# Group-norm rows, fox groups, state matmuls and merged rows put at other places of one unit order

## The chip, the cores and the metric

The kernel runs as one program on one core of a Trainium2 chip. The metric is device time of the execution in microseconds (us), lower is better. The engines of the core are called here as the profile calls them: PE (TensorE, matmul), PEld (its weight loads), DVE (VectorE), ACT (ScalarE), POOL (GpSimd) and SP (SyncE, which issues all DMAs of this kernel).

## The reference, cut to what matters

Two different blocks run one after the other on 256 tokens of width 1024, each two layers deep.

```python
def first_block(...):                      # per layer
    proj = h @ w_in[layer]                 # x_bc, z, dt, q, k, v, ... , gates
    y_a = mamba2_branch(...)               # state-space scan, then grouped_rms_norm
    y_b = sliding_window_branch(...)       # "swa"
    y_c = forgetting_attention_branch(...) # "fox": scores + cum[q] - cum[k], causal softmax
    merged = sum_i sigmoid(gate_i) * (y_i @ w_proj[layer, i])
    x = x + merged @ w_out[layer]
def merge_branches(...):                   # second block, per layer
    y = g_a * (o_attn @ w_br_attn) + g_p * (pool @ w_br_pool) + g_f * (fourier @ w_br_four)
    return y @ w_out
def conv_ffn(h, w_up, conv_w, w_down): ...
```

## The kernel before, in words

**Arithmetic.** Every large product is made of float32 rounded to its high part and the remainder: `W = hi + lo`, `x = xh + xl`, and three matmuls (`hi*xh`, `hi*xl`, `lo*xh`; L797 to L799 when the weights stand still, L810 to L812 when tokens do). Weights come as half chunks of 128x1024. SP loads a half chunk into one of seven `raw` buffers (L728), ACT copies it into `hi` (L1145), and DVE (L1454) or POOL (L1925) subtracts to get `lo`. There are five `hi`/`lo` pairs (`NS = 5`), so the `split` of half chunk i+5 stands in the order next to the matmuls that read half chunk i, and ACT's copy waits until PE has used half chunk i. A chunk for 256 tokens is 48 matmuls.

**Order.** One Python object writes a list of units by hand. All five engines walk this same list, each does its own part of each unit, in order, and waits by semaphore. `gemm` appends: the split of a later half chunk, the matmul unit, another split, and then one `tick()`. A tick advances every generator in `self.side` by one step; this is how the narrow work (attention groups, state-space groups, group norm) is laid between the weight chunks. So a unit that waits on one engine holds all that stands behind it in the list on that engine, the weight splits too.

**What the change touches.** The fox generator `attn("fox", l, g)` takes eight ticks: `fox_prep` at 0, `scores` 2, `exp` 3, `probs` 4, `turn` (transposes of the probabilities) 6, `pv` 7. Before, group g was appended after its v chunk, so groups 0 to 3 start at ticks 3, 6, 9 and 12 of the layer (tick 0 is the first q chunk; q, k and v chunks fill ticks 0 to 11, the eight conv chunks 12 to 19). In `fox_prep` SP first waits for the splits that stand before it in the list (it must issue their successors' loads in order), then issues a broadcast read `t_A<-cu_scratch` of 512 KB (L748); POOL waits for it and does two subtractions (L1932, L1933) and two selects (L1919). Groups use two buffers in turn.

State-space groups (`ssm`) start at ticks 0, 2, 6 and 8 of a later stretch. `ssm0` copies, `ssm1` has exponentials on ACT and waits for a broadcast read too, `ssm2` is three multiplications on DVE (L1636, then L1640 twice), `ssm3` is the state matmul and its copy on ACT (L1267), `ssm4` the output matmuls (L966 to L968), which need that copy.

Group norm: `gnorm` puts four `gn` units on DVE (L1681 and L1685). Then `ysplit` rounds the rows of each chunk: ACT copies (L1285), DVE subtracts (L1675). The projection `proj` of branch 0 reads them (k rows 0-1 are of chunk 0, and so on). In that stretch the last swa groups still run: `exp` of group 3, `turn` and `pv` of groups 2 and 3 (L1240 and L1608 copy out the transposes, L933 is `pv`).

In the second block, `msplit2` rounds the eight rows of the merged sum (ACT L1407, DVE L1851) into `H2`, which the gate matmuls read until the last gate chunk has passed, so all wait for that. `wout2` reads them.

Of the kernel before, what the change touches and what calls it, by code (L numbers as in the profile page):

```python
# [152 lines left out]
class Order:  # L153
# [145 lines left out]
    def ssm(self, l, g):  # L299
        self.add("ssm0", l=l, c=g, s=(self.sbank(), self.sbank()))  # L300
        yield
        self.add("ssm1", l=l, c=g)
        yield
        self.add("ssm2", l=l, c=g)
        yield
        yield
        self.add("ssm3", l=l, c=g, s=(self.sbank(),))
        yield
        self.add("ssm4", l=l, c=g, s=(self.sbank(),))

# [51 lines left out]
    def gated_proj(self, l, br, perm, split):  # L362

        def gate(c):
            self.gemm("gate", l, c, wcols("w_in", l, O_G + br * 1024 + np.arange(c * 256, c * 256 + 256)), 8, 256, 256,
                      x=(br,))

        def proj(c):
            self.gemm("proj", l, c, wcols("w_proj", (l, br), np.arange(c * 256, c * 256 + 256), perm), 8, 256, 256,
                      x=(br,))  # L370
        gate(0)
        gate(1)
        proj(0)
# [12 lines left out]
    def layer1(self, l):
        b = self.rstd(l, (2, 1, 1) if l else (0, 1, 1))
        self.add("norm1", l=l, g=b, n=(self.half(0), self.half(1)))
        self.late_splits()
        self.small(l)  # L390
        self.share = False
        for g in range(4):
            for off, kind in ((O_QC, "q"), (O_KC, "k")):
                self.gemm(kind, l, g, wcols("w_in", l, off + np.arange(g * 256, g * 256 + 256)), 8, 256, 256)
            self.vproj(l, "vc", O_VC, g)
            self.side.append(self.attn("fox", l, g))
            if l == 1 and g == 1:
                self.add("ctx")
        for n, c in enumerate((4, 6, 5, 7, 0, 1, 2, 3)):
            if l == 1 and n == 4:  # L400
                self.side.append(self.squares(8))
            self.gemm("conv", l, c, wcols("w_in", l, O_XBC + np.arange(c * 256, c * 256 + 256)), 8, 256, 256,
                      then=lambda m: self.later("conv2", l=l, c=c) or ())
        self.drain()
        self.share = True
        self.side.append(self.staggered([self.ssm(l, g) for g in range(4)], (0, 2, 6, 8)))
        self.zgate(l, 2, O_ZC, None)
        for c in range(4):
            self.gemm("rope", l, c, wcols("w_in", l, O_QB + SWA_PERM[c * 256:c * 256 + 256]), 8, 256, 256,
                      then=lambda m: self.rope_then(l, c))  # L410
        self.gemm("rope", l, 4, wcols("w_in", l, O_KB + np.arange(256)), 8, 256, 256,
                  then=lambda m: self.rope_then(l, 4))
        self.vproj(l, "vb", O_VB, 0)
        rest = self.gated_proj(l, 2, None, False)
        next(rest)
        self.drain()
        self.side.append(self.staggered([self.attn("swa", l, g) for g in range(4)], (0, 2, 5, 7)))
        self.zgate(l, 0, O_ZA, None)
        for _ in rest:
            pass  # L420
        for c in range(4):
            self.add("ysplit", l=l, c=c, x=(0,))
        for _ in self.gated_proj(l, 0, None, False):
            pass
        self.drain()
        self.zgate(l, 1, O_ZB, SWA_PERM)
        for _ in self.gated_proj(l, 1, SWA_PERM, True):
            pass
        self.add("msplit", l=l, c=3)
        self.tick()  # L430
        self.some_mods(1)
        every, self.every = self.every, 0
        self.side.append(self.squares(l + 1))
        for c in range(4):
# [50 lines left out]
    def block2(self, l):  # L485
# [34 lines left out]
        for bi, nkt, wn, perm in ((1, 2, "w_br_pool_2", None), (2, 2, "w_br_four_2", None), (0, 4, "w_br_attn_2", LAT_PERM)):  # L520
            for c in range(4):
                self.gemm("gate2", l, c, wcols("w_in_2", l, 1280 + bi * 1024 + np.arange(c * 256, c * 256 + 256)), 8, 256,
                          tw, x=(bi, tw))
                if bi == 0 and c == 0:
                    self.drain()
                if bi == 0 and c == 3:
                    for k in range(6):
                        self.add("msplit2", l=l, c=k)
                self.gemm("proj2", l, c, wcols(wn, l, np.arange(c * 256, c * 256 + 256), perm), nkt, 256, tw,
                          x=(bi, tw, nkt, len(units)))  # L530
# [72 lines left out]
class Tiles:  # L603
# [78 lines left out]

    def attn(self, kind, l, g):

        o = (5120 if kind == "fox" else 2048) + 1536 * (g % 2)
        f = self.a if kind == "fox" else self.b
        t0 = f(o, 512).rearrange("p (h c) -> p h c", h=4)
        t1 = f(o + 512, 1024).rearrange("p (h c) -> p h c", h=4)
        base = self.ST[:, (g % 2) * 64:(g % 2) * 64 + 64]
        return t0, t1, [base[:, 8 * i:8 * i + 8] for i in range(5)]  # L690

    def ssm(self, g):
# [72 lines left out]
def tensor(e, units, t, M):  # L765
# [318 lines left out]
    def proj2(u):  # L1084
        bi, tw, nkt, n = u.x[2:]
        k0 = (0, 4, 6)[bi]
        chan(u, nkt, 256, tw, lambda k: t.Y2[:, k0 + k, 0:tw], lambda k: t.YL2[:, k0 + k, 0:tw],
             lambda k: at("y2", u.l, k0 + k), ("proj2mm", u.l))

    def wout2(u):  # L1090
        tw = 256 if u.l else 512
        chan(u, 8, 256, tw, *h2(tw), lambda k: at("m2", u.l, k), ("wout2mm", u.l))

    def ffup(u):
        tw = 256 if u.l else 512
# [29 lines left out]
def scalar(e, units, t, M):  # L1125
# [21 lines left out]
    def sq(u):  # L1147
        s = u.l
        tw, c0 = (256, 256) if s == 8 else (256, 0) if s == 3 else (TW[s], 0)
        for k in (u.c, u.c + 1):  # L1150
# [252 lines left out]

    def msplit2(u):
        tw = 256 if u.l else 512
        q.wait_ge(at("mg2", u.l, 0, u.c), at("h2mm", u.l, 0))
        act(t.H2[:, u.c, 0:tw], t.M2[:, u.c, 0:tw], ACT.Copy).then_inc(*up("act", ("m2h", u.l, u.c), ("m2", u.l, u.c), ("m2", u.l)))  # L1407

    def ffup(u):
        l, pr, vg, tw = u.l, u.c, u.x[2], 256 if u.l else 512  # L1410
# [27 lines left out]
def vector(e, units, t, M):  # L1438
# [409 lines left out]
    def msplit2(u):  # L1848
        tw = 256 if u.l else 512
        q.wait_ge(at("m2h", u.l, u.c))  # L1850
        tt(t.HL2[:, u.c, 0:tw], t.M2[:, u.c, 0:tw], t.H2[:, u.c, 0:tw].bitcast(F), ALU.subtract).then_inc(  # L1851
            *up("dve", ("m2", u.l, u.c), ("m2", u.l)))

    def xadd(u, s, j, k, ps):
# [59 lines left out]
def gpsimd(e, units, t, M):  # L1914
# [249 lines left out]
```

## Time and profile before

| what | value |
|---|---|
| median of 3 runs | 2228.97 us (2228.39 to 2231.36) |
| the profiled execution, own time | 2235.63 us |
| its span, first to last instruction | 2233.9 us |
| PE busy | 2100.3 us (94%) |
| PEld, DVE, ACT, POOL busy | 1865.8, 1258.7, 1107.3, 958.7 us |
| mean granted PE clock | 0.972 |
| HBM read | 327.08 MB, 147 GB/s over the span |

A busy PE is near the bound of the kernel, so what matters is the 6% in which it is not busy, and the stretches in which its granted clock is below 1.

### The profile page before, as it was taken

What the parts mean: (1) busy time and instruction counts of PE and PEld (TensorE: products, weight loads), DVE (VectorE), ACT (ScalarE), POOL (GpSimd) and SP (SyncE); (2) the same over time, 40 slices, a digit from 0 to 9 for tenths busy, and PEclk for the clock granted to TensorE, in tenths of its full rate; (3) what the DMA queues carried; (4) which work ended last, traced back from release to release, by engine and by line L of the source; (5) the groups of instructions that cost most, each with busy time, mean ns of one, the idle gap of its engine ahead of it and who ended that gap; (6) DMA issues with size and microseconds to landing.
All of it is one profiled execution on the core that took longest, in us unless ns stands there. A gap on an engine that the chain in (4) does not pass through costs nothing.

```text
span 2233.9 us, 36649 instructions
## 1 busy us (share of the span) xinstructions
PE 2100.3 (94%) x14868; PEld 1865.8 (84%) x14868; DVE 1258.7 (56%) x1902; ACT 1107.3 (50%) x1873; POOL 958.7 (43%) x426
## 2 busy tenths in 40 slices
PE   5999998999999998998999999899999979999997
PEld 5898997998998998996766787678888868898997
DVE  5576847336477655454276435555445546856665
ACT  4475466545575475544266323433333345646553
POOL 3564644563546644652111333323333333365663
PEclk9999999999999999998999999999999989999998
DMA  6445443566554543565112343433333313354551
GB/s 234 179 157 178 160 150 125 188 208 220 204 191 154 185 146 125 192 204 188 67 66 86 127 142 121 169 125 109 129 113 132 106 64 104 116 180 140 196 180 60
DMA packets 93176, 330.64 MB, mean 148 GB/s; under 512 B 10064, under 2 KB 13264, under 8 KB 92752
## 3 DMA queue, kind: packets, MB, share of 16 engines
q1 hardware_dynamic: 93008, 328.30, 42.7%
q8 instruction: 118, 1.93, 0.3%
q14 instruction: 50, 0.41, 0.1%
HBM read 327.08 MB, written 1.18 MB: 147 GB/s over the span
## 4 chain that ended last, share of the span: by engine, by line
PE 79%; DVE 10%; ACT 7%; issue 2%; POOL 1%; DMA 1%; SPq 0%; DVEq 0%; ACTq 0%; POOLq 0%
PE ps L797 22%; PE ps L798 21%; PE ps L799 21%; ACT t_hi L1145 2%; PE ps L844 2%; PE ps L810 1%; PE ps L811 1%; PE ps L812 1%; DVE t_lo L1454 1%; PE ps L933 1%; PE ps L1059 1%; PE ps L917 1%; DVE t_RB L1829 1%; PE ps L1069 1%; ACT t_B L1231 1%
## 5 line engine op out<-in xcount | busy, mean ns | idle before, releaser
L1925 POOL TENSOR_TENSOR t_lo<-t_raw,t_hi 128x1024 fp32r<-128x1024 f32 (+1 forms) x358 | 878.6, 2463 | 1078.6 <-ACT t_hi L1145 1070.5
L797 PE MATMUL ps<-t_RB,t_hi 128*128 128x256 f32 (+1 forms) x3712 | 1173.8, 316 | 20.5 <-DVE t_RB L1741 5.3
L798 PE MATMUL ps<-t_RB,t_hi 128*128 128x256 f32 (+1 forms) x3712 | 1151.2, 310 | 0.0
L799 PE MATMUL ps<-t_RB,t_lo 128*128 128x256 f32 (+1 forms) x3712 | 1150.5, 310 | 0.0
L797 PEld LDWEIGHTS ps<-t_RB,t_hi 128*128 128x128 f32 x3712 | 714.8, 193 | 94.2 <-issue 31.2
L798 PEld LDWEIGHTS ps<-t_RB,t_hi 128*128 128x128 f32 x3712 | 715.4, 193 | 34.9 <-issue 2.0
L799 PEld LDWEIGHTS ps<-t_RB,t_lo 128*128 128x128 f32 x3712 | 714.6, 192 | 35.8
L1145 ACT ACTIVATE t_hi<-t_raw 128x1024 fp32r<-128x1024 f32 (+1 forms) x506 | 524.5, 1042 | 426.9 <-PE ps L799 389.8
L1454 DVE TENSOR_TENSOR t_lo<-t_raw,t_hi 128x1024 fp32r<-128x1024 f32 x148 | 207.3, 1402 | 288.7 <-ACT t_hi L1145 288.5
L1884 DVE SCALAR_TENSOR_TENSOR t_A<-ps,t_V,t_A 128x510 f32<-128x510 f32 (+1 forms) x176 | 102.3, 612 | 154.6 <-ACT t_A L1415 153.1
L1415 ACT ACTIVATE t_A<-ps,t_V 128x512 f32<-128x512 f32 (+1 forms) x88 | 48.5, 577 | 125.9 <-PE ps L799 125.9
L810 PE MATMUL ps<-t_hi,t_RB 128*128 128x256 f32 (+1 forms) x320 | 94.9, 296 | 11.1 <-DVE t_RB L1741 7.2
L1857 DVE SCALAR_TENSOR_TENSOR t_X<-ps,t_MOD,t_X 128x256 f32<-128x256 f32 x168 | 72.0, 478 | 58.9 <-PE ps L799 58.9
L811 PE MATMUL ps<-t_hi,t_RB 128*128 128x256 f32 (+1 forms) x320 | 91.9, 287 | 0.0
L812 PE MATMUL ps<-t_lo,t_RB 128*128 128x256 f32 (+1 forms) x320 | 91.7, 287 | 0.0
L810 PEld LDWEIGHTS ps<-t_hi,t_RB 128*128 128x128 f32 x320 | 63.0, 197 | 18.1 <-DVE t_RB L1741 8.1
L1464 DVE TENSOR_TENSOR t_SQA<-t_SQA,t_NT 128x256 f32<-128x256 f32 (+1 forms) x63 | 52.6, 834 | 29.6 <-ACT t_NT L1166 26.0
L811 PEld LDWEIGHTS ps<-t_hi,t_RB 128*128 128x128 f32 x320 | 63.4, 198 | 0.3 <-issue 0.2
L812 PEld LDWEIGHTS ps<-t_lo,t_RB 128*128 128x128 f32 x320 | 63.3, 198 | 0.0
L1401 ACT ACTIVATE t_A<-ps 128x512 f32<-128x512 f32 (+1 forms) x48 | 22.4, 490 | 81.6 <-PE ps L799 78.3
L844 PE MATMUL ps<-t_raw,t_C 128*32 128x256 f32 x768 | 55.2, 409 | 4.7 <-DVE t_X L1857 2.6
L1427 ACT ACTIVATE t_RB<-t_A 128x512 fp32r<-128x512 f32 (+1 forms) x44 | 23.2, 526 | 70.6 <-DVE t_A L1899 70.6
(302 smaller groups left out, 2180.5 us busy)
## 6 DMA issues: line engine op xcount, KB each, us to landing
t_raw<-in_W SPq DMA_DIRECT2D x586, 512.0 KB, 3.5
t_A<-cu_scratch SPq DMA_DIRECT2D x8, 512.0 KB, 6.1
t_B<-cu_scratch SPq DMA_DIRECT2D x8, 512.0 KB, 4.7
t_raw<-in_W SPq DMA_DIRECT2D x16, 256.0 KB, 2.9
t_A<-in_C SPq DMA_DIRECT2D x2, 1536.0 KB, 8.6
t_X<-in_X SPq DMA_DIRECT2D x2, 512.0 KB, 4.4
t_X<-in_X SPq DMA_DIRECT2D x1, 1024.0 KB, 9.9
out<-t_X SPq DMA_DIRECT2D x1, 1024.0 KB, 4.8
```

What stands on the lines that cost most here:

```text
L797: mm(o, hi[:, w], xh(k), start=k == 0 and j == 0, stop=False)
L798: mm(o, hi[:, w], xl(k), start=False, stop=False)
L799: i = mm(o, lo[:, w], xh(k), start=False, stop=k == nkt - 1 and m == u.x[1] - 1)
L810: mm(o, xh(k)[:, r], hi[:, w], start=k == 0 and j == 0, stop=False)
L811: mm(o, xl(k)[:, r], hi[:, w], start=False, stop=False)
L812: i = mm(o, xh(k)[:, r], lo[:, w], start=False, stop=k == nkt - 1 and tb == blocks[-1])
L844: i = mm(b[32 * j:32 * j + 32, 0:256], t.C32[:, k, :], t.raw[r % NR][:, j * 256:j * 256 + 256], start=k < 4, stop=k >= 4)
L1145: act(t.hi[s][:, 0:w], t.raw[r][:, 0:w], ACT.Copy).then_inc(*up("act", ("hi", u.i), ("split", u.i)))
L1454: tt(t.lo[s][:, 0:w], t.raw[r][:, 0:w], t.hi[s][:, 0:w].bitcast(F), ALU.subtract).then_inc(*up("dve", ("split", u.i)))
L1857: stt(out=x, in0=ps[:, z * 256:z * 256 + 256], scalar=t.modv(u.l, j, k, z), in1=x, op0=ALU.mult, op1=ALU.add).then_inc(*up("dve", ("x", s, ...
L1884: return stt(out=o[:, :, r], in0=ps[:, :, s], scalar=cw, in1=o[:, :, r], op0=ALU.mult, op1=ALU.add)
L1925: tt(t.lo[s][:, 0:w], t.raw[r][:, 0:w], t.hi[s][:, 0:w].bitcast(F), ALU.subtract).then_inc(*up("pool", ("split", u.i)))
```

## The change

Five edits of the order and of places in memory, no edit of the arithmetic:

1. The four `ysplit` units of branch 0 stood together ahead of gate chunk 0. Now rows 0 and 1 stand after gate chunk 0 and rows 2 and 3 after gate chunk 1, both ahead of projection chunk 0.
2. Fox groups start at ticks 4, 6, 9 and 11 (before 3, 6, 9 and 12). Group 2 gets a third buffer, in `RS` and `NT`, and the small sums move to fit; the buffer of group g is now waited for as that of group g-3.
3. `ssm3` stands one tick earlier; `ssm4` keeps its tick.
4. `msplit2` of rows 0 and 1 goes ahead of projection chunk 2 of the attention branch, 2 to 5 ahead of chunk 3. Rows 0 to 3 are written to `Y2`/`YL2` places 4 to 7 (pool and Fourier rows lay there), so they wait only for branch 2 to be done.
5. Squares of tensor 8 wait for the transposes of fox group 2 of layer 1, whose buffer they share.

```diff
@@ ssm
         self.add("ssm2", l=l, c=g)
         yield
+        self.add("ssm3", l=l, c=g, s=(self.sbank(),))
         yield
-        self.add("ssm3", l=l, c=g, s=(self.sbank(),))
         yield
         self.add("ssm4", l=l, c=g, s=(self.sbank(),))
@@ gated_proj
-        gate(0)
-        gate(1)
+        for i in range(2):
+            gate(i)
+            if br == 0:
+                self.add("ysplit", l=l, c=2 * i, x=(0,))
+                self.add("ysplit", l=l, c=2 * i + 1, x=(0,))
         proj(0)
@@ layer1
+        self.side.append(self.staggered([self.attn("fox", l, g) for g in range(4)], (4, 6, 9, 11)))
         for g in range(4):
...
-            self.side.append(self.attn("fox", l, g))
...
-        for c in range(4):
-            self.add("ysplit", l=l, c=c, x=(0,))
@@ block2
-                if bi == 0 and c == 3:
-                    for k in range(6):
+                if bi == 0 and c > 1:
+                    for k in range(2 * c - 4, 2 * c - 2 if c == 2 else 6):
                         self.add("msplit2", l=l, c=k)
@@ Tiles.attn
-        o = (5120 if kind == "fox" else 2048) + 1536 * (g % 2)
+        n = g % (3 if kind == "fox" else 2)
+        o = (5120 if kind == "fox" else 2048) + 1536 * n
+        t0, t1 = (self.RS[:, :], self.NT[:, :]) if n == 2 else (f(o, 512), f(o + 512, 1024))
-        base = self.ST[:, (g % 2) * 64:(g % 2) * 64 + 64]
+        base = self.ST[:, n * 40:n * 40 + 40]
@@ Tiles
+    def split_of_m(self, k, tw):
+        hi, lo, k = (self.Y2, self.YL2, 4 + k) if k < 4 else (self.H2, self.HL2, k)
+        return hi[:, k, 0:tw], lo[:, k, 0:tw]
@@ scalar: sq, msplit2
-                q.wait_ge(at("ctx"))
+                q.wait_ge(at("ctx"), at("turned", "fox", 1, 2))
-        q.wait_ge(at("mg2", u.l, 0, u.c), at("h2mm", u.l, 0))
+        q.wait_ge(at("mg2", u.l, 0, u.c), at("branch2", u.l, 2) if u.c < 4 else at("h2mm", u.l, 0))
@@ gpsimd: fox_prep
-        q.wait_ge(at("bc", l, g), at("smallc", l), was("turned", "fox", l, g - 2), was("layer", l - 1))
+        q.wait_ge(at("bc", l, g), at("smallc", l), was("turned", "fox", l, g - 3), was("layer", l - 1))
```

## Rows read from the trace of the kernel before

**Rows 1.** Waits of PE, whole span: us in total, times, longest us
```profile
PE ps L829 <- DVE t_SQA L1464: 35.0, 8, 15.6
PE ps L933 <- ACT t_B L1240: 8.7, 3, 7.0
PE ps L966 <- ACT t_B L1267: 6.0, 2, 4.1
PE ps L797 <- DVE t_RB L1851: 3.3, 2, 2.1
```

**Rows 2.** Busy time by stretch: PE, PEld, DVE, ACT, POOL; granted clock, DMA share, GB/s
```profile
345.00:400.00 55.00, 44.50 (x365) 41.15 (x363) 35.37 (x44) 31.20 (x66) 21.24 (x9) 0.91 0.33 109
214.00:235.00 21.00, 19.13 (x148) 17.64 (x147) 19.15 (x20) 9.03 (x13) 13.16 (x6) 0.92 0.55 186
584.00:604.00 20.00, 17.11 (x124) 16.50 (x122) 10.88 (x12) 9.62 (x25) 11.06 (x7) 0.83 0.53 202
400.00:450.00 50.00, 50.00 (x417) 50.00 (x418) 17.72 (x18) 25.98 (x32) 29.71 (x13) 1.00 0.58 197
```

**Rows 3.** Timeline of PE at its stalls: start us, us, engine, line, idle before
```profile
366.30 0.39 PE L797 MATMUL ps<-t_RB,t_hi 128*128 128x256 f32 x1 [2.99 <-DVE t_RB L1675]
381.39 1.12 PE L933 MATMUL ps<-t_B,t_A 128*64 128x256 f32 x4 [7.52 <-DVE t_ST L1598]
...
867.33 1.12 PE L933 MATMUL ps<-t_B,t_A 128*64 128x256 f32 x4 [7.01 <-ACT t_B L1240]
```

**Rows 4.** Timeline of ACT in the group-norm stretch of layer 0
```profile
363.10 0.63 ACT L1285 ACTIVATE t_RB<-t_A 128x512 fp32r<-128x512 f32 x1 [9.97 <-DVE t_A L1685]
...
379.32 1.08 ACT L1240 ACTIVATE t_B<-ps 128x512 f32<-128x512 f32 x2
```

**Rows 5.** Timeline of DVE there
```profile
350.08 2.38 DVE L1685 SCALAR_TENSOR_TENSOR t_A<-t_A,t_V,t_T 128x256 f32<-128x256 f32 x2
...
364.76 0.88 DVE L1685 SCALAR_TENSOR_TENSOR t_A<-t_A,t_V,t_T 128x256 f32<-128x256 f32 x2
...
379.46 1.23 DVE L1454 TENSOR_TENSOR t_lo<-t_raw,t_hi 128x1024 fp32r<-128x1024 f32 x1 [11.41 <-ACT t_hi L1145]
...
381.64 2.69 DVE L1602 TENSOR_TENSOR t_B<-t_B,t_ST 128x512 f32<-128x512 f32 x1
```

**Rows 6.** Timeline of PE at the state-space stalls, both layers
```profile
223.68 0.40 PE L966 MATMUL ps<-t_B 128*64 128x128 f32 x2 [1.87 <-ACT t_B L1267]
...
712.21 0.45 PE L966 MATMUL ps<-t_B 128*64 128x128 f32 x2 [4.12 <-ACT t_B L1267]
```

**Rows 7.** Timeline of ACT, and of DVE, ahead of the second of them
```profile
695.67 0.41 DVE L1636 TENSOR_TENSOR t_B<-t_B,t_SM 128x256 f32<-128x256 f32 x1
...
710.37 0.58 ACT L1314 ACTIVATE t_T<-ps 128x512 f32<-128x512 f32 x1
```

**Rows 8.** Timeline of PE at the fox stalls
```profile
100.31 0.35 PE L797 MATMUL ps<-t_RB,t_hi 128*128 128x256 f32 x1 [3.08 <-POOL t_lo L1925]
...
180.24 0.69 PE L933 MATMUL ps<-t_B 128*64 128x256 f32 x2 [2.53 <-ACT t_hi L1145]
...
593.86 0.87 PE L917 MATMUL ps<-t_C,t_A 128*128 128x128 f32 x3 [2.90 <-DVE t_A L1577]
```

**Rows 9.** Timeline of POOL around fox groups 1 and 2 of layer 0
```profile
91.36 1.04 POOL L1932 TENSOR_TENSOR t_A<-t_E,t_A 128x512 f32<-128x512 f32 x1 [8.58 <-DMA t_A<-cu_scratch]
...
126.18 2.38 POOL L1925 TENSOR_TENSOR t_lo<-t_raw,t_hi 128x1024 fp32r<-128x1024 f32 x1 [0.31 <-ACT t_hi L1145]
```

**Rows 10.** The broadcast reads of L748, from issue to landing
```profile
DMA to landing us min/median/max: 4.2/6.1/11.8
```

**Rows 11.** Timeline of DVE where merged rows are rounded, layers 0 and 1
```profile
1348.17 5.22 DVE L1851 TENSOR_TENSOR t_RB<-t_A,t_RB 128x512 fp32r<-128x512 f32 x6 [9.55 <-ACT t_RB L1407]
...
1354.03 2.62 DVE L1846 TENSOR_TENSOR t_A<-t_A 128x512 f32<-128x512 f32 x1
...
1989.71 6.25 DVE L1851 TENSOR_TENSOR t_RB<-t_A,t_RB 128x256 fp32r<-128x256 f32 x6 [3.73 <-ACT t_RB L1407]
```

More of the change, by code:

```diff
@@ L683, in attn @@
     def attn(self, kind, l, g):
-        o = (5120 if kind == "fox" else 2048) + 1536 * (g % 2)
+        n = g % (3 if kind == "fox" else 2)
+        o = (5120 if kind == "fox" else 2048) + 1536 * n
         f = self.a if kind == "fox" else self.b
-        t0 = f(o, 512).rearrange("p (h c) -> p h c", h=4)
-        t1 = f(o + 512, 1024).rearrange("p (h c) -> p h c", h=4)
-        base = self.ST[:, (g % 2) * 64:(g % 2) * 64 + 64]
+        t0, t1 = (self.RS[:, :], self.NT[:, :]) if n == 2 else (f(o, 512), f(o + 512, 1024))
+        t0, t1 = (x.rearrange("p (h c) -> p h c", h=4) for x in (t0, t1))
+        base = self.ST[:, n * 40:n * 40 + 40]
         return t0, t1, [base[:, 8 * i:8 * i + 8] for i in range(5)]
@@ L1087, in proj2 @@
         chan(u, nkt, 256, tw, lambda k: t.Y2[:, k0 + k, 0:tw], lambda k: t.YL2[:, k0 + k, 0:tw],
-             lambda k: at("y2", u.l, k0 + k), ("proj2mm", u.l))
+             lambda k: at("y2", u.l, k0 + k), ("proj2mm", u.l), ("branch2", u.l, bi))
     def wout2(u):
         tw = 256 if u.l else 512
-        chan(u, 8, 256, tw, *h2(tw), lambda k: at("m2", u.l, k), ("wout2mm", u.l))
+        ms = [t.split_of_m(k, tw) for k in range(8)]
+        chan(u, 8, 256, tw, lambda k: ms[k][0], lambda k: ms[k][1], lambda k: at("m2", u.l, k), ("wout2mm", u.l))
     def ffup(u):
@@ L1405, in msplit2 @@
         tw = 256 if u.l else 512
-        q.wait_ge(at("mg2", u.l, 0, u.c), at("h2mm", u.l, 0))
-        act(t.H2[:, u.c, 0:tw], t.M2[:, u.c, 0:tw], ACT.Copy).then_inc(*up("act", ("m2h", u.l, u.c), ("m2", u.l, u.c), ("m2", u.l)))
+        q.wait_ge(at("mg2", u.l, 0, u.c), at("branch2", u.l, 2) if u.c < 4 else at("h2mm", u.l, 0))
+        act(t.split_of_m(u.c, tw)[0], t.M2[:, u.c, 0:tw], ACT.Copy).then_inc(*up("act", ("m2h", u.l, u.c), ("m2", u.l, u.c), ("m2", u.l)))
     def ffup(u):
@@ L1850, in msplit2 @@
         q.wait_ge(at("m2h", u.l, u.c))
-        tt(t.HL2[:, u.c, 0:tw], t.M2[:, u.c, 0:tw], t.H2[:, u.c, 0:tw].bitcast(F), ALU.subtract).then_inc(
+        hi, lo = t.split_of_m(u.c, tw)
+        tt(lo, t.M2[:, u.c, 0:tw], hi.bitcast(F), ALU.subtract).then_inc(
             *up("dve", ("m2", u.l, u.c), ("m2", u.l)))
```

## The prediction

> **What bounds the kernel now.** I read the page's first two parts, then the waits of PE, then every PE stall over 0.15 us on the timeline with what released it, then the other engines ahead of each stall. PE is busy 94% of the span, at 0.12 us a matmul where nothing disturbs it (400 to 450: 417 matmuls in 50.0 us) [rows 2]. So the matmuls can't be made faster by any of these edits. What can be won is PE's idle time, 124 us, and the time in which PE runs at its lower clock after an idle stretch. The waits [rows 1] say how much of the idle the edits touch. 35.0 us are the waits for the root mean square (L829), which no edit touches. The edits touch 8.7 us on L933, 6.0 us on L966, 3.3 us on L797 behind L1851, and single stalls of the fox groups and the projection.
>
> The clock counts beside the idle. For a stretch I take (1 − granted clock) x length: 0.08 x 21 = 1.7 us around one state-space stall, 0.09 x 55 = 5.0 us around group norm, 0.17 x 20 = 3.4 us around a fox stall [rows 2]. Part of this lies inside the idle itself and isn't counted twice below.
>
> **The group-norm rows.** Before, ACT takes rows 0 and 1, then stands 9.97 us at row 2, which needs DVE's third `gn`, and 1.95 us at row 3 [rows 4]. Behind it in ACT's list stand four copies of weights, two gate evictions, the exponentials of swa group 3 and the copies of `turn` group 2, which run only at 379.32 [rows 4]. PE pays with 2.99 us at 366.30, where DVE's subtraction of row 0 comes late, and 7.52 us at 381.39, where `pv` of group 2 waits for that copy [rows 3]. In layer 1 the second stall is 7.01 us [rows 3].
>
> The edit takes ACT past this. It doesn't move the first stall: DVE's fourth `gn` ends at 364.76 + 0.88 = 365.6 [rows 5], and rows 0 and 1 stand behind it on DVE before and after, so the projection still starts at about 366.3. What changes is rows 2 and 3. They now stand behind gate chunk 1 with, on DVE, one weight split (1.23), one transposed copy (some 0.7) and `probs` of group 3 (2.69 plus small ones) ahead [rows 5]; before, DVE had none of these until 379.46, idle for 11.41 us. From 366.9 that is 1.2 + 0.7 + 3.2 + 2 waits between them and row 2 itself, so about 374.4, and row 3 at 375. The projection runs its first 24 matmuls by some 370 and stalls some 4 to 5 us in its middle; its last quarters then end at 377.4. The copies of `turn` are long done, so `pv` starts at 377.4 instead of 381.39, 4.0 us earlier. In layer 1 the same working gives 864.1 instead of 867.33, 3.2 us. The stall in the middle is shorter than that before, so some clock comes back, 1.3 us in both together. Against it: POOL's splits, which ACT's copies now release early, run while DVE does the `gn`s. The pair L1685 took 2.38 us at 350.08 and 0.88 at 364.76 [rows 5]; one such slip in each layer costs 1.5 us. I take 3.5 + 3.5 = **7 us** gained; bounds 2 (two slips a layer and the stall full) and 11 (rows 2 and 3 find DVE free, stall of the middle gone but 0 to 1 us).
>
> The Trainium skill ("SBUF — State Buffer", "Who interferes with whom") says that a VectorE instruction with two SBUF inputs and a GpSimd one that reads SBUF exclude each other for the whole instruction, the first to start winning. The pair above agrees: 1.50 us longer, of a split of 2.38. By that rule alone every `gn` pair could slip by up to a split, which is the rival named port below; the sum above doesn't need it.
>
> **The state matmul a tick earlier.** `ssm3`'s copy (L1267) stood on ACT behind the next group's `ssm1`, which waits for its broadcast read. So `ssm4` stalled 1.87 us in layer 0 and 4.12 us in layer 1 [rows 6]. A tick earlier the copy is ahead of that `ssm1`: some 12 us of slack. Each stall also cost 1.7 us of clock [rows 2]. Layer 0: 1.87 + 1.7 = 3.6. Layer 1: 4.12 + 1.7 = 5.8, less two new waits. `ssm3` at about 695.4 needs the product L1636, which runs from 695.67 for 0.41 [rows 7]: 0.8. And ACT's L1314 at 710.37 [rows 7], which the held list delayed, now meets a rope that wants it some 1.1 us sooner than it can be. So 3.9. The other groups' `ssm3` find `ssm2` done one tick (5.8 us) back, so they cost nothing; with DVE late by more than a tick they would cost what it is late. Sum **7.5 us**, bounds 5 and 9.3.
>
> **Fox ticks and third buffer.** What stalls here are the weight splits of POOL that stand behind `fox_prep`. Before, the preparation of group 1 had POOL idle 8.58 us for its broadcast read, and the split behind it came 3.08 us late for PE [rows 8, 9]. The reads take 4.2, 6.1 and 11.8 us at the least, median and most [rows 10]. They are not made faster. Only places change: group 0 and group 3 swap splits with their neighbours. Layer 0: the 3.08 becomes 1.5 to 3 (POOL's preparation meets less of DVE's work); group 0 now stands ahead of one more split, needed at about 84 and ready 82.7 to 84.4, so 0 to 0.5 lost; group 3's preparation now stands ahead of the split that ran at 126.18 for 2.38 [rows 9], which is then ready at 141 to 143 and needed at 141.1, so 0.2 to 2.1 lost. The last `pv`, 2.53 late behind DVE's and ACT's lists [rows 8], comes a tick later relative to its transposes and isn't late: 2.53 + 1.3 of clock gained. Net +2. Layer 1: the 2.90 at the transposes of group 0 [rows 8] and its clock, 2.90 + 2.5 = 5.4 in all, give way to a wait for a split behind the preparation of group 1, of 2.4 to 3.7 with its clock: +1.5. Sum **3.5 us**. Upper bound 7 (no new wait), lower bound −4: one split more held by a read of the slowest kind, 11.8 − 6.1 = 5.7, with 1.7 of clock, which turns 3.5 into −4. The third buffer alone is worth nothing where `turned` of two groups back is long past; it lets the groups stand two ticks apart.
>
> **Merged rows.** DVE rounds six rows in 5.22 us ahead of the multiply L1846, which itself takes 2.62 where POOL's split runs (L1685's pair showed the same size of slip) [rows 11]. Now two rows go a chunk earlier: 2 x 0.87 = 1.7 less, of which the rows' own readiness leaves 1.2. PE's two waits there sum to 3.3 [rows 1]. Layer 0 +1.2 (0.5 to 2.5); layer 1 with 6.25 for six [rows 11], 2 x 1.04 less, +1.0 (0.8 to 2.6). Sum **2.2 us**, bounds 1.3 and 4.5 (the upper one with the clock). Rows 0 to 3 in other places cost nothing: the branch 2 that they wait for ended chunks before.
>
> **The squares' wait** costs nothing: ACT's own copies for `turn` of group 2 stand ahead in its list, and tick 15 is unchanged for it; if DVE's half were late, 0.7 us.
>
> **The sum.** 7 + 7.5 + 3.5 + 2.2 = 20.2 us; the bounds add to 4.3 and 31.8. The profiled execution took 2235.63 us (span 2233.9), 6.7 above the median 2228.97; so 2215.4 for an execution like it, and 2228.97 − 20.2 = about **2209 us** for the median.
>
> **The rivals.**
> *The fox ticks give back.* A read at three of the moved places lands between the median and the slowest, and the next split on POOL comes late as before. For it: all four reads of the old order held POOL, 8.58 us at one of them [rows 9], and no edit shortens them. Against: the splits run five half chunks ahead. Gain 5 to 13, about 2219 us.
> *The port.* POOL's splits fall onto DVE's `gn` and `scores`, two slips of 1.50 [rows 5] a layer, and row 2 comes as late as the old `pv`: the first part is worth nothing, gain 13, 2216 us.
> *No change.* Each stall's replacement is as long as the stall; gain under 4.5 us, 2226 to 2229. For it: PE's idle is only what DVE, ACT and POOL are behind, and nothing is taken off them.
> *Slower: late reads.* The broadcast read lands near 11.8 us [rows 10] at the sites where it now stands ahead of one split more (groups 0, 1 and 3 of layer 0, group 1 of layer 1): each holds that split 11.8 − 6.1 = 5.7 us, and PE with it, with 1.7 of clock: 4 x 7.4 = 29.6 against 20.2, so 2238 us. It decides from a fourth site: three at 7.4 are 22.2, which only eats the gain. Against: 11.8 is the slowest of all, and the median is half of it.
>
> **How the numbers follow.** The forecast as summed (gain 13 to 27) 0.58; fox gives back 0.20; port 0.10; no change 0.08; slower 0.04. 0.2% is 4.5 us, about what a measurement of this kernel can tell from no change. Faster is 0.58 + 0.20 + 0.10 = 0.88, same 0.08, slower 0.04. The range: 2202 (gain 27) to 2222 (gain 7) leaves out the no-change and slower cases (0.12) and the edges of the others (0.07).
>
> **What the profile after would show.** PE's waits: L966 behind L1267 near zero; L933 behind L1240 gone, and in its place a wait of L797 for L1675 in the middle of the projection of some 4 us a layer; ACT's 9.97 idle gone; the stall before the projection, 2.99, still there. Around fox group 1 of layer 1 a wait of L797 for POOL's L1925. L1851's 3.3 down to some 1.5. Granted clock of 345 to 400 at 0.93 or more. Wrong if: the middle stall is 7 us (DVE's list fuller than counted) or absent; the stall behind the third fox preparation passes 3 us; new waits of PE on L1925 sum to more than 8 us.

## The result

| kernel | median, us | lowest to highest | runs |
|---|---|---|---|
| before | 2228.91 | 2228.39 to 2231.36 | 6 |
| changed | 2238.27 | 2234.76 to 2241.49 | 6 |

The ratio of the times is 1.0041 (95% interval 1.0028 to 1.0054): the change makes the kernel 9 us slower, where 20 us faster was forecast, and the range of 2202 to 2222 us doesn't hold it. The profiled execution of the changed kernel took 2240.19 us, with a span of 2238.5 us. Its page says that the engines do what they did:

```profile
PE 2098.5 (94%) x14868; PEld 1864.1 (83%) x14868; DVE 1272.8 (57%) x1902; ACT 1105.6 (49%) x1873; POOL 957.1 (43%) x426
```

PE is busy 1.8 us less than before in a span that is 4.6 us longer, so the time is in what PE waits for. (DVE is busy 14.1 us more, with the same number of instructions.) In the changed kernel the lines of before are seven to nine further down: L829 is L836, L797 to L799 are L804 to L806, L933 is L940, L966 is L973, POOL's split L1925 is L1934, the row subtraction L1675 is L1683, L1851 is L1860. The waits of PE over the whole span, in us in total, times, and longest us, to be read against [rows 1]:

```profile
PE ps L836 <- DVE t_SQA L1472: 35.5, 8, 15.0
PE ps L804 <- DVE t_RB L1683: 15.8, 5, 5.2
PE ps L804 <- POOL t_lo L1934: 10.8, 2, 5.5
PE ps L940 <- DVE t_ST L1608: 8.0, 2, 5.1
...
PE ps L804 <- DVE t_RB L1860: 3.4, 4, 1.5
...
PE ps L965 <- DVE t_B L1644: 2.0, 2, 1.4
PE ps L940 <- ACT t_B L1248: 1.7, 2, 0.9
```

The 6.0 us of the state-space stalls are gone, as forecast, and so are the waits of `pv` of the swa groups: 8.7 us behind ACT are 1.7, and the 7.5 us behind DVE at 381.39 [rows 3] are 0. Three other rows have come: 15.8 us for the group-norm rows (3.0 before), 10.8 us for weight splits of POOL (3.3 before) and 8.0 us for `pv` of fox group 2, which never waited before. The single stalls on PE's timeline:

```profile
101.97 0.55 PE L804 MATMUL ps<-t_RB,t_hi 128*128 128x256 f32 x1 [5.33 <-POOL t_lo L1934]
...
164.76 1.12 PE L940 MATMUL ps<-t_B 128*64 128x256 f32 x4 [5.14 <-DVE t_ST L1608]
...
370.29 0.58 PE L804 MATMUL ps<-t_RB,t_hi 128*128 128x256 f32 x1 [5.22 <-DVE t_RB L1683]
...
380.15 0.58 PE L804 MATMUL ps<-t_RB,t_hi 128*128 128x256 f32 x1 [5.06 <-DVE t_RB L1683]
...
597.32 0.55 PE L804 MATMUL ps<-t_RB,t_hi 128*128 128x256 f32 x1 [5.46 <-POOL t_lo L1934]
...
653.28 0.65 PE L940 MATMUL ps<-t_B 128*64 128x256 f32 x4 [2.81 <-DVE t_ST L1608]
...
868.62 0.39 PE L804 MATMUL ps<-t_RB,t_hi 128*128 128x256 f32 x1 [4.13 <-DVE t_RB L1683]
```

Each is followed by matmuls at the lower clock. The windows around them (columns as in [rows 2]) have granted clocks of 0.86, 0.83 and 0.88:

```profile
90.00:115.00 25.00, 19.67 (x150) 18.94 (x152) 10.10 (x11) 13.80 (x40) 13.54 (x8) 0.86 0.46 171
155.00:175.00 20.00, 14.86 (x111) 13.70 (x110) 12.74 (x20) 13.24 (x25) 7.31 (x3) 0.83 0.40 132
345.00:400.00 55.00, 44.73 (x353) 42.65 (x353) 36.34 (x46) 30.56 (x66) 21.90 (x9) 0.88 0.35 114
```

**A ledger by stretch.** PE runs the same matmuls in nearly the same order in all these kernels. So I took the start on PE of the same chunk in two traces, and the growth of the difference from one such chunk to the next is what a stretch gained (−) or lost (+) against the kernel before. It holds idle and clock together. The short stretches between those listed are left out, so a column doesn't add to the whole.

| stretch, us against before | changed | ticks_old | early_old | rows_four | best |
|---|---|---|---|---|---|
| fox, layer 0 | +5.9 | −1.9 | −5.4 | −4.6 | −7.6 |
| state space, layer 0 | −3.5 | −3.5 | −3.4 | −3.5 | −3.4 |
| group norm, layer 0 | +0.3 | −0.3 | −0.2 | −6.6 | −7.1 |
| fox, layer 1 | +7.8 | +0.2 | −5.8 | −1.6 | −5.6 |
| state space, layer 1 | −2.4 | −1.8 | −2.1 | −2.1 | −1.9 |
| group norm, layer 1 | −2.9 | −2.2 | −2.4 | −9.1 | −9.1 |
| block two, layer 0 to `wout2` | −1.6 | −1.2 | −1.3 | −1.3 | +0.7 |
| block two, layer 1 to `wout2` | +3.3 | +2.7 | +2.7 | +3.4 | 0.0 |

The other columns are experiments below. Every number compares one trace with one trace, and kernels with the same order in a stretch show how far that carries. The fox stretch of layer 0 is the same in ticks_old, rows_old, state_old, merge_old and rows_four: −1.9, −2.2, −2.4, +0.1 and −4.6. four_alone, which has the old order there, has −2.0, and state_old, which has the old state matmul, has −1.7 and +1.1 in the state-space stretches. So differences of some 3 us between single traces, in that stretch 5, mean little unless a named stall stands behind them. The runs of most kernels spread over 5 to 9 us. For the whole of a kernel the ratios are what counts.

### The profile page after: what moved, and what is told of

It is laid out like the page before. It is cut to its first block, busy times and chain, and to the rows that moved or that the text cites. A ratio compares the mean times of both kernels' runs of the same rounds, so it can differ in the third digit from the quotient of the medians.

```text
span 2238.5 us, 36656 instructions
## 1 busy us (share of the span) xinstructions
PE 2098.5 (94%) x14868; PEld 1864.1 (83%) x14868; DVE 1272.8 (57%) x1902; ACT 1105.6 (49%) x1873; POOL 957.1 (43%) x426
## 4 chain that ended last, share of the span: by engine, by line
PE 75%; DVE 13%; ACT 7%; issue 2%; DMA 1%; POOL 1%; SPq 0%; DVEq 0%; ACTq 0%; POOLq 0%
PE ps L804 21%; PE ps L805 20%; PE ps L806 20%; ACT t_hi L1153 2%; PE ps L851 2%; DVE t_lo L1462 2%; PE ps L817 1%; PE ps L818 1%; PE ps L819 1%; PE ps L1066 1%; PE ps L940 1%; POOL t_lo L1934 1%; DVE t_RB L1683 1%; DVE t_RB L1860 1%; DVE t_SQA L1472 1%
## 5 line engine op out<-in xcount | busy, mean ns | idle before, releaser
L1934 POOL TENSOR_TENSOR t_lo<-t_raw,t_hi 128x1024 fp32r<-128x1024 f32 (+1 forms) x358 | 879.9, 2467 | 1090.8 <-ACT t_hi L1153 1077.0
L804 PE MATMUL ps<-t_RB,t_hi 128*128 128x256 f32 (+1 forms) x3712 | 1174.2, 316 | 40.4 <-DVE t_RB L1683 15.8
L806 PE MATMUL ps<-t_RB,t_lo 128*128 128x256 f32 (+1 forms) x3712 | 1152.2, 310 | 0.0
L804 PEld LDWEIGHTS ps<-t_RB,t_hi 128*128 128x128 f32 x3712 | 716.8, 193 | 115.1 <-issue 39.4
L806 PEld LDWEIGHTS ps<-t_RB,t_lo 128*128 128x128 f32 x3712 | 716.5, 193 | 35.7
```

Source lines behind the costliest of these rows:

```text
L804: mm(o, hi[:, w], xh(k), start=k == 0 and j == 0, stop=False)
L806: i = mm(o, lo[:, w], xh(k), start=False, stop=k == nkt - 1 and m == u.x[1] - 1)
L1934: tt(t.lo[s][:, 0:w], t.raw[r][:, 0:w], t.hi[s][:, 0:w].bitcast(F), ALU.subtract).then_inc(*up("pool", ("split", u.i)))
```

## The experiments

Theory after the result: the new ticks of the fox groups lose 11 to 14 us, and the other edits still gain. (The first expectation has 5.4 us for layer 1, where the table has 7.8: it ends one chunk earlier, ahead of a stall of 1.03 us, and starts at another chunk.) Rivals: the third buffer, or one of the other edits. Each kernel was timed beside the kernel before, on the same chip; the ratio is to it. There were three chips, so ratios compare between rows, and medians need not.

| kernel | median, us | lowest to highest | ratio | 95% interval |
|---|---|---|---|---|
| ticks_old | 2224.33 | 2222.78 to 2228.13 | 0.9974 | 0.9966 to 0.9983 |
| ticks_g3 | 2236.43 | 2232.28 to 2239.28 | 1.0027 | 1.0017 to 1.0037 |
| ticks_g0 | 2228.32 | 2224.86 to 2231.29 | 0.9991 | 0.9982 to 1.0000 |
| read_early | 2227.14 | 2224.05 to 2231.25 | 0.9980 | 0.9971 to 0.9990 |
| rows_old | 2224.13 | 2219.68 to 2228.84 | 0.9976 | 0.9964 to 0.9987 |
| state_old | 2229.60 | 2224.79 to 2233.20 | 0.9999 | 0.9987 to 1.0010 |
| merge_old | 2223.40 | 2220.36 to 2229.70 | 0.9969 | 0.9958 to 0.9981 |
| rows_four | 2209.86 | 2205.32 to 2210.18 | 0.9906 | 0.9890 to 0.9923 |
| g3_exp_late | 2225.65 | 2223.00 to 2228.24 | 0.9978 | 0.9967 to 0.9988 |
| early_old | 2212.19 | 2208.49 to 2217.82 | 0.9917 | 0.9904 to 0.9930 |
| best | 2200.32 | 2198.61 to 2201.14 | 0.9861 | 0.9847 to 0.9875 |
| four_alone | 2214.20 | 2210.70 to 2217.81 | 0.9922 | 0.9910 to 0.9934 |

A difference of two ratios times 2229 us is given below as the price of what differs between two kernels; with intervals this wide it is good to some 3 us.

**ticks_old.** The changed kernel with one edit taken back.

```diff
-        self.side.append(self.staggered([self.attn("fox", l, g) for g in range(4)], (4, 6, 9, 11)))
+        self.side.append(self.staggered([self.attn("fox", l, g) for g in range(4)], (3, 6, 9, 12)))
```

> The changed kernel with fox groups at ticks 3, 6, 9, 12 again; the third buffer stays. Theory: the new ticks are what made the change slower. Comparing the two traces unit by unit, the fox stretches took 5.9 us more in layer 0 and 5.4 us more in layer 1. So with the old ticks about 2238.3 - 11.3 = 2227 us, slightly faster than the kernel before (2228.9), and the stalls of 5.33 and 5.46 us behind POOL's weight split and of 5.14 and 2.81 us at pv of group 2 are gone. Rival: the third buffer, or the places of RS and NT, cost it: then it stays near 2238. Second rival: the part lost is in the other edits; then it is between 2232 and 2238.

0.9974 against 1.0041: the ticks cost 14.9 us, and the ledger puts 7.8 and 7.6 into the two fox stretches. The third buffer, which is still in it, costs nothing that shows. What is left of the change is 6 us faster than before.

**ticks_g3 and ticks_g0.** Only one of the two ticks moved: (3, 6, 9, 11) and (4, 6, 9, 12).

> Ticks 3, 6, 9, 11: only group 3 starts a tick earlier. Theory: the exponentials of group 3 now stand ahead of the transposes of group 2 in ACT's and DVE's lists, so that the copies of the transposes come late and pv of group 2 stalls (5.14 and 2.81 us in the changed kernel), and no wait for POOL's split beyond the old 3.08 us. About 2227 + 6 = 2233 us. Rival: the stall at pv of group 2 came only because everything before it had been pushed by group 0: then pv of group 2 doesn't stall and the time is that of the old ticks, 2227.

> Ticks 4, 6, 9, 12: only group 0 starts a tick later. Theory: fox_prep of group 0 then runs between two weight splits that SP waits for before it issues the broadcast read of group 1, so that read goes out some 2.5 us later and PE waits 5.3 us for the split behind it in layer 0 (3.08 before) and as much in layer 1 (where a stall of 2.90 at the transposes goes away). About 2227 + 5 = 2232 us, pv of group 2 without a stall. Rival: the two ticks only hurt together; then 2227.

Group 3 alone costs 0.53% or 11.8 us, group 0 alone 0.17% or 3.8 us, where the intervals just touch; together 15.6 against 14.9, so they add within the error. The stalls are where the theory has them. In ticks_g3 `pv` of group 2 stalls in both layers on PE's timeline; in ticks_g0 it doesn't, and the row of PE's waits for POOL's splits is large instead.

```profile
161.83 0.65 PE L940 MATMUL ps<-t_B 128*64 128x256 f32 x4 [3.63 <-DVE t_ST L1608]
...
647.56 1.12 PE L940 MATMUL ps<-t_B 128*64 128x256 f32 x4 [2.80 <-DVE t_ST L1608]
```

```profile
PE ps L804 <- POOL t_lo L1934: 8.9, 2, 5.0
```

For group 0 that row was 2.9 us in ticks_old, so 6.0 us have come; against them the waits at the transposes (L924) fell from 4.8 to 1.5 us, which leaves 2.7 us. The fox stretches of its trace are together as long as those of ticks_old, so the place of the 3.8 us is shown by the stalls alone.

The two theories had both sizes at 5 to 6 us. Group 3's is twice that. Its trace, of an execution with 2230.8 us span, lies at the low end of its runs, and that of ticks_old at the high end; the two fox stretches show some 9 of the 12 us. Where the rest is isn't known.

**g3_exp_late.** In ticks_g3 the exponentials of group 3 and what follows go back by one tick.

```diff
         self.add("scores", l=l, c=g, s=(self.sbank(), self.sbank(), self.sbank()), x=(kind,))
         yield
+        if kind == "fox" and g == 3:
+            yield
```

> Ticks 3, 6, 9, 11 as in ticks_g3 (2236.4 us), but the exponentials of group 3 and all behind them one tick later, as late as with ticks 3, 6, 9, 12; only preparation and scores of group 3 stay a tick early. Theory: it is the exponentials, standing ahead of the transposed copies of group 2 in ACT's list, that make pv of group 2 stall (3.6 and 2.8 us in ticks_g3, with lower clock after each). With them behind again both stalls are gone: 2224 to 2227 us. Rival: the early scores hurt, since they stand directly behind the probabilities of group 2 on DVE and the preparation stands ahead of weight split 30 on POOL (1.27 us of PE's wait in ticks_g3): then 2230 or more.

2225.65: 10.9 of the 11.8 us come back with this one tick. So it is the place of the exponentials or of what stands behind them, not that of the preparation or the scores. The run moves the probabilities, `turn` and `pv` of group 3 too; that it is the exponentials is read from the traces. How it works is seen in the changed kernel on ACT, and then on DVE:

```profile
148.81 1.28 ACT L1238 ACT_TABLE_LOAD   x1
152.78 0.40 ACT L1238 ACTIVATE t_A<-t_A,t_ST 128x128 f32<-128x128 f32 x1 [2.68 <-DVE t_ST L1599]
...
161.04 1.08 ACT L1248 ACTIVATE t_B<-ps 128x512 f32<-128x512 f32 x2
```

```profile
143.01 2.67 DVE L1610 TENSOR_TENSOR t_RS<-t_RS,t_ST 128x512 f32<-128x512 f32 x1
145.60 3.42 DVE L1611 TENSOR_TENSOR t_NT<-t_NT,t_ST 128x1024 f32<-128x1024 f32 x1
...
160.24 2.69 DVE L1668 SCALAR_TENSOR_TENSOR t_A<-ps,t_V,t_A 128x255 f32<-128x255 f32 x6 [3.77 <-ACT t_A L1212]
...
163.97 0.69 DVE L1616 COPY t_B<-ps 128x512 f32<-128x512 f32 x1
```

DVE does the probabilities of group 2 (L1610, L1611), then the scores of group 3, which end late; ACT stands 2.68 us for their row sums, then does the exponentials, and only then all that stands behind them: two weight copies, a conv eviction (L1212), and at 161.04 its two transposed copies of group 2. The third copy is DVE's (L1616). It stands behind the additions of the conv chunk (L1668), for which DVE waits 3.77 us until ACT has made that eviction, and behind a split, so it starts at 163.97. PE had made the transposes by 153.86, and waits for this last copy until 164.76. With the old order ACT's copies came first: in ticks_old at 153.83, and the exponentials of group 3 at 156.81. The prediction went wrong here by looking at the tick of `turn` for each group and not at what one group's `exp` passes in another's list. Two shorter stalls remain in g3_exp_late (2.77 and 1.80 us, its own trace), so a bit is left to the early scores; the time can't tell.

```profile
157.68 0.65 PE L942 MATMUL ps<-t_B 128*64 128x256 f32 x4 [2.77 <-issue]
...
639.95 0.65 PE L942 MATMUL ps<-t_B 128*64 128x256 f32 x4 [1.80 <-ACT t_A L1241]
```

**read_early and early_old.** SP's list is reordered: `fox_prep` of group 1 goes ahead of the three weight loads before it. read_early is the changed kernel with this, early_old is ticks_old with it.

```diff
+def earlier_reads(units):
+    out = list(units)
+    for u in units:
+        if u.kind == "fox_prep" and u.c == 1:
+            i = next(n for n, v in enumerate(out) if v is u)
+            out.pop(i)
+            k = 3
+            while k:
+                i -= 1
+                k -= out[i].kind in ("split", "mod")
+            out.insert(i, u)
+    return out
 def sync(e, units, t, M):
     rows = [(u, h) for u in units for h in range({"split": 1, "mod": 2}.get(u.kind, 0))]
+    units = earlier_reads(units)
```

> The changed kernel, with the broadcast read of fox group 1 in both layers issued three weight loads earlier in SP's list. Theory: it lands some 4 us earlier, POOL's split behind the preparation of group 1 too, so the stalls of 5.33 and 5.46 us shrink to 0 to 2 us: about 2238.3 - 8 = 2230 us. Rival: POOL has no time for the preparation earlier, since it does the splits 16 and 18 until 86 us, or the weight loads that now stand behind the read come late: then within 3 us of 2238.

> ticks_old (2224.3 us) with the broadcast read of fox group 1 issued three weight loads earlier. Theory: the stall of 2.93 us behind POOL's split 20 in layer 0 goes, with its half clock, and in layer 1 the wait at the transposes of group 0 shrinks: 4 to 6 us faster, about 2219. Rival: with the old ticks POOL has its preparation late for other reasons and the loads behind the read are late: no gain, 2224.

It gives 13.6 us to the changed kernel and 12.7 us to ticks_old, more than expected. So it also takes away waits that the kernel before had, and its size is not that of the new ticks' fault. First the changed kernel, on SP and on POOL:

```profile
82.69 4.17 SPq L735 DMA_DIRECT2D t_raw<-in_W  x4
86.91 1.29 SPq L755 DMA_DIRECT2D t_A<-cu_scratch  x1
```

```profile
76.19 1.04 POOL L1941 TENSOR_TENSOR t_A<-t_E,t_A 128x512 f32<-128x512 f32 x1 [8.06 <-DMA t_A<-cu_scratch]
...
80.22 5.76 POOL L1934 TENSOR_TENSOR t_lo<-t_raw,t_hi 128x1024 fp32r<-128x1024 f32 x2
93.04 1.04 POOL L1941 TENSOR_TENSOR t_A<-t_E,t_A 128x512 f32<-128x512 f32 x1 [7.06 <-DMA t_A<-cu_scratch]
...
98.51 5.65 POOL L1934 TENSOR_TENSOR t_lo<-t_raw,t_hi 128x1024 fp32r<-128x1024 f32 x2
```

POOL's two splits at 80.22 stand behind the preparation of group 0 and end at 85.98. SP can't load into their `raw` buffers earlier, and the read of group 1 stands behind these loads, so it goes out at 86.91; in the kernel before it went out at 84.40. POOL then idles 7.06 us, prepares group 1, and has split 20 ready 3.3 us after 98.51; PE waits 5.33 us. Now read_early, SP and then POOL:

```profile
82.25 0.43 SPq L770 DMA_DIRECT2D t_A<-cu_scratch  x1
```

```profile
87.14 1.04 POOL L1956 TENSOR_TENSOR t_A<-t_E,t_A 128x512 f32<-128x512 f32 x1 [1.99 <-DMA t_A<-cu_scratch]
...
92.17 4.76 POOL L1949 TENSOR_TENSOR t_lo<-t_raw,t_hi 128x1024 fp32r<-128x1024 f32 x2
```

The read goes out 4.7 us earlier, POOL idles 1.99 us instead of 7.06, and PE has no wait there at all. In layer 1 the preparation starts at 573.70 instead of 590.80. There two things are better: the read goes out at 566.86 instead of 580.42, ahead of two transfers of the context (`t_X<-in_X`, `t_C<-in_C`) and not behind them, and it lands after 3.4 us instead of 10.3 (11.8 in the kernel before). So in layer 0 the cost of group 1's `fox_prep` is set by where SP stands when it issues the read, in layer 1 by the shorter landing too. The run doesn't separate these two, and that the context's transfers made the landing long isn't shown. A new stall takes some of it back in read_early, behind the preparation of group 3, and early_old hasn't got it:

```profile
142.25 0.58 PE L819 MATMUL ps<-t_RB,t_hi 128*128 128x256 f32 x1 [4.58 <-POOL t_lo L1949]
```

The kernel before had the stall at group 1 as well [rows 8]: early_old takes 3.5 us from the fox stretch of layer 0 and 6.0 from that of layer 1, against ticks_old.

**rows_old, state_old, merge_old.** ticks_old with one of the other edits undone in each: the four `ysplit` ahead of gate chunk 0; `ssm3` on its old tick; the six `msplit2` together ahead of chunk 3.

```diff
@@ rows_old
-        for i in range(2):
-            gate(i)
-            if br == 0:
-                self.add("ysplit", l=l, c=2 * i, x=(0,))
-                self.add("ysplit", l=l, c=2 * i + 1, x=(0,))
+        gate(0)
+        gate(1)
...
+        for c in range(4):
+            self.add("ysplit", l=l, c=c, x=(0,))
@@ state_old
-        self.add("ssm3", l=l, c=g, s=(self.sbank(),))
         yield
+        self.add("ssm3", l=l, c=g, s=(self.sbank(),))
@@ merge_old
-                if bi == 0 and c > 1:
-                    for k in range(2 * c - 4, 2 * c - 2 if c == 2 else 6):
+                if bi == 0 and c == 3:
+                    for k in range(6):
```

> The kernel ticks_old (the changed one with fox ticks 3, 6, 9, 12; 2224.3 us) with the four group-norm rows ahead of gate chunk 0 again, as before the change. Theory: the new places gave nothing in layer 0 (0.3 us between the traces: the two stalls of 2.99 and 7.52 us became two of about 5.2 and 5.1) and 2.2 to 2.9 us in layer 1. So some 2.5 us slower than ticks_old, about 2227. Rival: my forecast of 3.5 us a layer holds and the trace misled me: 2231. Other rival: nothing at all, 2224.

> ticks_old with the state matmul back on its old tick. Theory: the stretch gained 3.5 us in layer 0 and 1.8 to 2.4 us in layer 1, where the state matmul now waits for DVE's product (1.4 us) and a gate chunk for a rope product (1.2 us). So 5.5 us slower than ticks_old, about 2230, with the stalls of 1.87 and 4.12 us back. Rival: the waits only move on to the rope and gate chunks and the whole is worth under 2 us: 2226.

> ticks_old with all six merged rows ahead of chunk 3 again. Theory: 1.2 us from layer 0 (its stall went from 2.15 to 0.82), and in layer 1 about nothing, so 1 us slower than ticks_old, 2225.5. Rival: in layer 1 the new order costs: between the traces the stretch from the square sums of block two's second layer to wout2 is 2.7 to 3.3 us longer in every version with the change. If the merged rows are the cause, this one is 2 us faster than ticks_old, 2222.

The group-norm rows are worth 0.4 us (0.9976 against 0.9974), the state matmul 5.6 us (0.9999), the merged rows −1.1 us (0.9969). Only the second is beyond the intervals. For the merged rows the ledger shows two parts: some −1.2 us in layer 0 and +2.7 to +3.4 in layer 1 in the kernels of the table that have the edit, 0.0 in `best`, which has not; but 1.1 to 1.5 in read_early, ticks_g3 and g3_exp_late, which have it too. Part of the latter is a lower clock at a place that stands ahead of the edit's instructions in layer 1 and has the same stall of 1.58 us in both, at 1888.28 in the changed kernel and at 1875.51 in merge_old. The two windows start 13.3 us ahead of it, first the changed kernel, then merge_old:

```profile
1875.00:1905.00 30.00, 28.17 (x185) 22.54 (x185) 25.02 (x46) 22.03 (x44) 12.04 (x6) 0.89 0.30 95
```

```profile
1862.23:1892.23 30.00, 28.07 (x210) 22.19 (x208) 26.99 (x52) 24.55 (x49) 12.06 (x6) 1.00 0.36 113
```

0.11 x 30 is 3.3 us. ticks_g3, which has the edit, has a clock of 1.00 there too. So the edit alone doesn't set it, and what decides between the two is open.

**rows_four and four_alone.** All four rows between gate chunks 0 and 1: rows_four is ticks_old with this, four_alone is the kernel before with nothing but this. The edit of four_alone:

```diff
         gate(0)
+        for r in range(4 if br == 0 else 0):
+            self.add("ysplit", l=l, c=r, x=(0,))
         gate(1)
         proj(0)
...
-        for c in range(4):
-            self.add("ysplit", l=l, c=c, x=(0,))
```

> ticks_old with all four group-norm rows between gate chunks 0 and 1 (the change has two there and two after gate chunk 1). Theory: in the changed kernel rows 2 and 3 stand on DVE behind a weight split, a transposed copy and the probabilities of swa group 3, and PE stalls 5.06 us (layer 0) and 4.13 us (layer 1) in the middle of the projection for them. In the new place they need only the last gn, so this stall goes, ACT's exponentials are already done, and pv of group 2 waits at most 1 us: 7 us faster than ticks_old, about 2217. Rival: the rows then hold ACT until the last gn is done, gate chunk 1 and the transposes' copies come late as in the kernel before, and pv of group 2 stalls 4 to 7 us: 2224 to 2227.

> The kernel before with one edit: the four group-norm rows stand between gate chunks 0 and 1. Theory: that place is worth the same in any of these kernels; rows_four was 14.5 us faster than ticks_old, and the traces put 13 of them into the two group-norm stretches (6.3 and 6.9). So 2229 - 14 = 2215 us. Rival: it needs the other edits (the earlier state copy gives ACT a different list): then 2220 to 2225.

rows_four is 15.2 us faster than ticks_old, four_alone 17.4 us faster than the kernel before (0.9922). What was wrong with two and two is seen on DVE in the changed kernel:

```profile
356.93 3.43 DVE L1611 TENSOR_TENSOR t_B<-t_B,t_ST 128x1024 f32<-128x1024 f32 x1
...
369.55 1.29 DVE L1683 TENSOR_TENSOR t_RB<-t_A,t_RB 128x512 fp32r<-128x512 f32 x2
373.35 1.22 DVE L1462 TENSOR_TENSOR t_lo<-t_raw,t_hi 128x1024 fp32r<-128x1024 f32 x1 [2.51 <-ACT t_hi L1153]
...
377.26 3.43 DVE L1683 TENSOR_TENSOR t_RB<-t_A,t_RB 128x512 fp32r<-128x512 f32 x2
```

Rows 0 and 1 are done at 370.8. Then DVE waits 2.51 us for ACT's copy for a split, does that, the transposed copy and the probabilities, and takes 3.43 us for rows 2 and 3, which took 1.29 us for rows 0 and 1: POOL's split ran beside it, from 376.35 to 379.54. In rows_four all four follow each other, on DVE, and PE has one stall and not two:

```profile
359.43 2.49 DVE L1682 TENSOR_TENSOR t_RB<-t_A,t_RB 128x512 fp32r<-128x512 f32 x4
```

```profile
360.17 0.58 PE L803 MATMUL ps<-t_RB,t_hi 128*128 128x256 f32 x1 [5.19 <-DVE t_RB L1682]
```

Its windows of nearly the same work have clocks of 0.94 and, in layer 1, 1.00 (0.88 in the changed kernel's layer 0, above):

```profile
330.00:385.00 55.00, 49.81 (x422) 47.04 (x420) 43.60 (x52) 35.88 (x72) 27.74 (x11) 0.94 0.43 137
830.00:865.00 35.00, 33.79 (x289) 32.37 (x288) 20.61 (x25) 22.59 (x44) 18.18 (x7) 1.00 0.45 151
```

So the ledger's 6.3 us (layer 0) and 6.9 us (layer 1) against ticks_old are the middle stall, 4.37 and 4.14 us in ticks_old, and the clock after it. The first stall stays: it is 5.21 us in four_alone as well.

**best.** rows_four with the merged rows together and the early read of group 1.

> rows_four (old fox ticks, four group-norm rows between gate chunks 0 and 1; 2209.9 us) with the six merged rows together again and the early read of fox group 1. Theory: the sum of the parts, 2209.9 - 1 - 4 = 2205 us. Rival: the gains of the early read are taken back by another wait: 2209.

2200.32 us, 1.4% or 31.0 us less than before, and 5 us more than forecast. The prices above (5.8 for ticks_old, 15.2, 12.7 and 1.1) sum to 34.8 us, so the parts nearly add.

## Why the prediction was wrong, point by point

**The fox ticks: the step that failed.** It was the term "Sum 3.5 us", with −4 as the lower bound; measured, the ticks cost 14.9 us. Two sentences in it were wrong. "group 0 now stands ahead of one more split ... so 0 to 0.5 lost": I priced the split and took the broadcast read of group 1 to be issued when it had been. But SP waits for the splits ahead of the read, so what delays a split delays the read, and POOL's next split with it: 5.33 us instead of 1.5 to 3 in layer 0, 5.46 in layer 1, before its clock, instead of 2.4 to 3.7 with it. ticks_g0 has stalls of 4.96 and 3.92 us there, and in read_early both are gone.

And for group 3 I listed POOL's split only, at 0.2 to 2.1 us. That its exponentials pass the transposed copies of group 2 in ACT's list was missing; it costs 5.14 and 2.81 us of stall and, with the lower clock after them, most of the 11.8 us (g3_exp_late).

Of the gains that I booked, the 2.90 us in layer 1 did come. The 2.53 us at the last `pv` are gone in the changed kernel, but they weren't the tick's to give. Of the ten traces with group 3 on its old tick, four have this stall (before, state_old, merge_old, early_old), and the other six have one of 1.2 to 1.5 us at the transposes of group 2 in its place. One of the six is four_alone, whose fox order is that of the kernel before. I had booked what one trace showed. Nor does the term follow from its own parts. They give 1.3 to 5.2 us for layer 0, where I took 2, and 1.7 to 3.0 for layer 1, where I took 1.5.

The rival "fox ticks give back" had the right place but the size for late landings. The landings were no later than before (median 6.0 us for 6.1, most 10.3 for 11.8); the issue was. The rival "slower" needed four reads of 11.8 us and was not what happened; that its 2238 us is the measured time is luck.

**The group-norm rows: mechanism right, size wrong.** I took 7 us; undone, the edit is worth 0.4, good to some 3. The end of the long ACT wait, the two stalls and their places came as told. The first stall was to stay at 2.99 and was 5.22, since the probabilities of group 2 met a split of POOL that now starts earlier. The multiplication L1611 took 3.43 us at 356.93, with the split on POOL from 356.36 to 359.27. In the kernel before, with POOL idle from 351.78 to 367.34, it took 1.22:

```profile
355.15 1.22 DVE L1603 TENSOR_TENSOR t_B<-t_B,t_ST 128x1024 f32<-128x1024 f32 x1
```

The 2.21 us between them are the 2.23 by which the first stall grew. The middle one was 5.06 where I had 4 to 5, starting 2 us later. That is the rival port: "row 2 comes as late as the old `pv`: the first part is worth nothing". It had a chance of 0.10, and put the slips on the `gn`s and scores; they fell on the probabilities and on rows 2 and 3. In layer 1, where the first stall was only 1.22 us, the ledger has 2.9 of the 3.5 forecast. By the Trainium skill ("SBUF — State Buffer", "Who interferes with whom") these pairs exclude each other, the first to start winning. The 3.43 against 1.22 us agrees with it: the split started 0.57 us ahead and DVE's instruction ended 1.1 us after it. One such slip cost 2.2 us, where I had priced 1.5.

**The state matmul: right.** Forecast 7.5, ledger 3.5 + 2.4 = 5.9, measured 5.6. Layer 0 came out at 3.5 for 3.6. In layer 1 the new wait for DVE's product was 1.43 us where I had 0.8 (row L965 of the waits, 2.0 us in two waits), and a gate chunk waits 1.2 us more. In ticks_old, to which the 5.6 belong, that wait is 2.96 us and the gate chunk has none.

**The merged rows: not confirmed.** In layer 0 the stall fell from 2.15 to 0.82 us, 1.3 for a forecast of 1.2. Layer 1, where I had +1.0, gave none of it: all of PE's waits for L1860 sum to 3.4 us, 3.3 before, where I had some 1.5. The edit as a whole is within the error of nothing.

**The signs.** I had named new waits of more than 8 us for POOL's splits as a sign of being wrong, and they are 10.8. The granted clock of 345 to 400 was to be 0.93 or more and is 0.88.

The sum by measured terms is 0.4 + 5.6 − 1.1 − 14.9 = −10 us, and the change measured −9; each term is good to some 3 us, so that they meet this closely is luck.

## What to carry to other kernels

When a unit is moved in a list that several engines walk, write down for each engine what it now passes, the DMA queue too. A wait there that doesn't look like the moved unit's own (SP waiting for a buffer that a split will free) is what moves the next transfer. Before a stall is booked as a gain, look for it in a second trace of the same order. Where one consumer stalls for late rows, try all rows together where their last input is ready: here, splitting them in two around another unit made two stalls of 5 us out of one.

## What was not expected of the hardware

A stall of PE can cost well over its own length: one of 2.93 us in ticks_old made its chunk last 11.51 us, and without the stall it lasted 6.01 us in early_old, 5.5 us for 2.93. The same stall of 1.58 us (1888.28 in the changed kernel) was followed by a granted clock of 1.00 in some kernels and of 0.89 in others with the same instructions there, over the 30 us windows shown. And the two multiplications of a group's probabilities, 0.69 and 1.22 us for an swa group (354.54 and 355.15 in the kernel before, POOL idle), took 2.67 and 3.42 us for a fox group of the changed kernel (143.01 and 145.60), with splits on POOL from 139.41 to 147.94.
